# First GEMM behind each norm with two weight panels (three in the differential layer) interleaved by k tile

## What is computed

```python
for l in range(DEPTH):                       # 4
    mod = silu(cond) @ w_mod[l] + b_mod[l]   # 6 vectors of 1024 per conditioning
    h = rmsnorm(x, g_norm1[l]) * (1 + mod[1]) + mod[0]
    x = x + mod[2] * mixer_l(h)              # 0 MLA, 1 differential, 2 GQA, 3 RG-LRU
    h = rmsnorm(x, g_norm2[l]) * (1 + mod[4]) + mod[3]
    gte, up = split(h @ w_ffn_in[l])         # 2 x 2816 columns
    x = x + mod[5] * ((silu(gte) * up) @ w_ffn_out[l])
```

## Time and profile before

| | |
|---|---|
| three runs | 3645.62, 3646.51, 3653.01 us |
| profiled execution, its time | 3648.95 us |
| its span | 3646.3 us |
| granted clock of TensorE, mean | 0.959 |
| PE busy | 3323.3 us (91%) |
| PE weight loads busy | 3018.5 us (83%) |
| DVE, ACT, POOL busy | 1915.9 (53%), 1115.1 (31%), 217.2 us (6%) |
| HBM | 298.49 MB read, 83 GB/s over the span |

### The profile page before, as it was taken

How to read it: one execution, slowest core, us unless ns; L and a number is a source line. 1 busy time by engine, 2 the same in 40 slices (tenths; PEclk the granted TensorE clock), 3 DMA queues, 4 the chain that set the end, 5 groups by cost and what they waited for, 6 DMA issues and landing times.

```text
span 3646.3 us, 53064 instructions
## 1 busy us (share of the span) xinstructions
PE 3323.3 (91%) x20320; PEld 3018.5 (83%) x20320; DVE 1915.9 (53%) x2728; ACT 1115.1 (31%) x1734; POOL 217.2 (6%) x120
## 2 busy tenths in 40 slices
PE   7978898999989998899999688899999776899999
PEld 2556677999987775799999566799999676899999
DVE  2133346757355665585844345575754688533332
ACT  1334433211134554321111334331111455321111
POOL 0311100000000000000000310000000342000000
PEclk9989999999999998999999899899999888999999
DMA  7300014443221110253522100163522211222222
GB/s 264 104 18 16 21 35 133 133 161 121 75 71 41 41 43 15 83 187 104 179 72 70 49 23 12 47 196 107 188 80 67 56 51 40 58 75 73 77 70 80
DMA packets 421859, 304.08 MB, mean 83 GB/s; under 512 B 12019, under 2 KB 389494, under 8 KB 421622
## 3 DMA queue, kind: packets, MB, share of 16 engines
q1 hardware_dynamic: 411412, 293.23, 26.2%
q10 hardware_dynamic: 10338, 9.41, 0.8%
HBM read 298.49 MB, written 4.10 MB: 83 GB/s over the span
## 4 chain that ended last, share of the span: by engine, by line
PE 81%; DVE 6%; ACT 6%; DVEq 2%; issue 2%; ACTq 1%; DMA 1%; SPq 0%
PE psB L295 29%; PE psA L295 29%; PE psD L295 7%; PE psC L358 3%; PE psA L339 2%; PE psC L311 2%; PE psC L350 2%; PE psB L339 2%; ACT h_hi L1339 1%; PE psA L729 1%; ACT work L1336 1%; DVE work L2216 1%; PE psB L729 1%; ACTq L1338 1%; ACT work L397 1%
## 5 line engine op out<-in xcount | busy, mean ns | idle before, releaser
L1357 ACT ACTIVATE w_hi<-raw 128x1024 fp32r<-128x1024 f32 (+1 forms) x307 | 317.3, 1035 | 1160.3 <-PE psB L295 766.3
L1870 DVE TENSOR_TENSOR w_lo<-raw,w_hi 128x1024 fp32r<-128x1024 f32 (+1 forms) x307 | 365.3, 1191 | 347.6 <-ACT w_hi L1357 347.1
L295 PE MATMUL psA<-h_hi,w_hi 128*128 128x320 f32 x1616 | 384.2, 320 | 71.9 <-DVE h_lo L1941 60.3
L295 PE MATMUL psA<-h_lo,w_hi 128*128 128x320 f32 x1616 | 375.2, 314 | 0.0
L295 PE MATMUL psA<-h_hi,w_lo 128*128 128x320 f32 x1616 | 375.1, 314 | 0.0
L295 PE MATMUL psB<-h_hi,w_hi 128*128 128x320 f32 x1616 | 368.4, 309 | 0.0
L295 PE MATMUL psB<-h_lo,w_hi 128*128 128x320 f32 x1616 | 368.2, 309 | 0.0
L295 PE MATMUL psB<-h_hi,w_lo 128*128 128x320 f32 x1616 | 368.2, 309 | 0.0
L295 PEld LDWEIGHTS psA<-h_hi,w_hi 128*128 128x128 f32 x1616 | 273.5, 192 | 91.8 <-issue 43.7
L1900 DVE SCALAR_TENSOR_TENSOR work<-work,silu_c 128x1024 f32<-128x1024 f32 x252 | 312.5, 1281 | 12.4 <-issue 0.9
L295 PEld LDWEIGHTS psA<-h_lo,w_hi 128*128 128x128 f32 x1616 | 277.0, 192 | 0.0
(11 more groups left out here) (288 smaller groups left out, 5367.6 us busy)
## 6 DMA issues: line engine op xcount, KB each, us to landing
raw<-in_w_ffn_in SPq DMA_DIRECT2D x176, 512.0 KB, 4.0
work<-in_w_mod SPq DMA_DIRECT2D x144, 512.0 KB, 4.8
raw<-in_w_ffn_out SPq DMA_DIRECT2D x64, 512.0 KB, 3.9
work<-in_w_mod SPq DMA_DIRECT2D x12, 2048.0 KB, 7.9
raw<-in_w_ffn_out SPq DMA_DIRECT2D x32, 384.0 KB, 3.4
raw<-in_diff_w_in SPq DMA_DIRECT2D x24, 512.0 KB, 3.8
raw<-in_lru_w_in SPq DMA_DIRECT2D x16, 512.0 KB, 4.6
raw<-in_gqa_w_in SPq DMA_DIRECT2D x12, 512.0 KB, 3.8
```

Of the source, the lines that this page charges most:

```text
L295: last = nc.tensor.matmul(out[:, b, 0:half], w[slot][:, kt * cols + c0:kt * cols + c0 + P], r[:, o:o + half], start=(kt == 0 and p == 0), ...
L1357: nc.scalar.activation(w_hi[s][:, 0:n], raw[s][:, 0:n], ACT.Copy).then_inc(hi_done, 1)
L1870: nc.vector.tensor_tensor(w_lo[s_][:, 0:n], raw[s_][:, 0:n], w_hi[s_][:, 0:n].bitcast(F32), ALU.subtract).then_inc(split_done, 1)
```

## The change

PE issues the same products. Where the GEMM stands behind a norm, its output tiles are taken together: for each k tile PE waits once for `h_done` and then does six products of the first tile, six of the second (and six of the third in the differential layer), each tile in its own PSUM tile and with its own weight slot. What each tile waited for (its panel, its PSUM tile) is now waited for ahead of the first product. In the differential layer q, k and v of head 0 go to psD, psA and psB, and the steps on q and k follow after all three; ACT reads k and v from there, and moves the high parts of the next head's panels ahead of `kout` and `kcache`. Nothing else moves: SP, POOL and DVE have the order they had.

```diff
+        def fresh_products(pe, tiles, n):
+
+            for _, _, before in tiles:
+                before()
+            last = [None] * len(tiles)
+            for kt in range(KT):
+                pe.wait_ge(h_done, n * KT + kt + 1)
+                for k, (out, slot, _) in enumerate(tiles):
+                    last[k] = products(pe, out, slot, KT, P, 0, h_hi, h_lo, 0, T, TH, range(kt, kt + 1))
+                    if kt == KT - 1:
+                        last[k].then_inc(gemm_done, 1)
...
-                    for t in range(6):
-                        if t >= 2:
-                            acts.wait(pe, f"m{t - 2}")
-                        h_tile(psum[t % 2], "mla_in", t // 2, t % 2, 0 if t == 0 else None).then_inc(gemm_done, 1)
+                    fresh_products(pe, [(psum[j], j, lambda j=j: take_panel(pe, "mla_in", 0, j)) for j in range(2)], 0)
+                    for t in range(2, 6):
+                        acts.wait(pe, f"m{t - 2}")
+                        h_tile(psum[t % 2], "mla_in", t // 2, t % 2).then_inc(gemm_done, 1)
...
                     h0 = Head(0, 0)
-                    gq(h0, 0, 8)
-                    gk(h0, 0, 2)
+                    fresh_products(pe, [(psum[(3, 0, 1)[j]], (2, 0, 1)[j],
+                                         lambda j=j: pe.wait_ge(split_done, phases["diff"].of_head(h0, j, 3)))
+                                        for j in range(3)], 2)
                     ssq(h0)
-                    gk(h0, 2, 8)
                     acts.wait(pe, "rsq", h0)
                     rotq(h0)
-                    gv(h0, 0, 2)
                     ssk(h0)
-                    gv(h0, 2, 5)
                     acts.wait(pe, "rsk", h0)
                     rotk(h0)
-                    gv(h0, 5, 7)
                     kturn(h0)
-                    gv(h0, 7, 8)
                     acts.wait(pe, "kcache", h0)
+                    acts.wait(pe, "evv", h0)
                     scores(h0, 0)
...
                     for j in range(2):
-                        h_tile(psA, "gqa_kv", j, 0, 4 if j == 0 else None).then_inc(gemm_done, 1)
-                        h_tile(psB, "gqa_kv", j, 1).then_inc(gemm_done, 1)
+                        if j == 0:
+                            fresh_products(pe, [(psum[k], k, lambda k=k: take_panel(pe, "gqa_kv", 0, k)) for k in range(2)], 4)
...
                     def block_products(i, fresh):
...
+                        if fresh is not None:
+                            fresh_products(pe, [(psum[j], (2, 0)[j], lambda j=j: take_panel(pe, "lru", 0, j))
+                                                for j in range(2)], fresh)
...
                     if ch == 0:
-                        hidden_tile(0, 2 * layer + 1)
+                        pe.wait_ge(silu_done, base + 1)
+                        pe.wait_ge(hidden_done, base + 1)
+                        pe.wait_ge(x_done, x_tiles[0])
+                        fresh_products(pe, [(psum[j], j, lambda j=j: take_panel(pe, f"in{layer}.0", 0, j))
+                                            for j in range(2)], 2 * layer + 1)
...
-                    for step in (cached, evq, rsq, evk, rsk, kout, kcache):
-                        step(h0)
+                    cached(h0)
+                    evq(h0)
+                    rsq(h0)
+                    evk(h0, psA)
+                    rsk(h0)
                     high(Head(0, 1), 0)
+                    kout(h0)
                     high(Head(0, 1), 1)
-                    evv(h0)
+                    kcache(h0)
+                    evv(h0, psB)
                     exp(h0, 0)
```

More of the change, by code:

```diff
@@ L277, in build, with products @@
         LRU_DVE = Steps(sem("lru_dve"), ["m", "u", "h", "g", "o"], 5)
-        def products(pe, out, slot, kts, cols, c0, rhs_hi, rhs_lo, at, stride, half, part=None,
-                     fresh=None, before_last=None):
+        def products(pe, out, slot, kts, cols, c0, rhs_hi, rhs_lo, at, stride, half, part=None, before_last=None):
             last = None
             for kt in part or range(kts):
-                if fresh is not None:
-                    pe.wait_ge(h_done, fresh * KT + kt + 1)
                 if before_last and kt == kts - 1:
@@ L815, in _, with h_tile @@
                 norm(2 * layer)
-                def h_tile(out, name, i, j, fresh=None):
+                def h_tile(out, name, i, j):
                     slot = take_panel(pe, name, i, j)
-                    return products(pe, out, slot, KT, P, 0, h_hi, h_lo, 0, T, TH, fresh=fresh)
+                    return products(pe, out, slot, KT, P, 0, h_hi, h_lo, 0, T, TH)
                 if layer == 0:
@@ L980, in project_head @@
                             pe.wait_ge(split_done, phases["diff"].of_head(h, j, 3))
-                        last = products(pe, psD, (2, 0, 1)[j], KT, P, 0, h_hi, h_lo, 0, T, TH, part,
-                                        fresh=2 if isinstance(h.i, int) and (h.i, h.k, j) == (0, 0, 0) else None)
+                        last = products(pe, psD, (2, 0, 1)[j], KT, P, 0, h_hi, h_lo, 0, T, TH, part)
                         if part[-1] == KT - 1:
@@ L986, in gq @@
                     def gq(h, k0, k1):
-                        if k0 == 0 and h is not h0:
+                        if k0 == 0:
                             acts.wait(pe, "evv", h.last())
@@ L1198, in block_products @@
                     def block_products(i, fresh):
-                        LRU_ACT.wait(pe, "trb", i - 1)
-                        h_tile(psA, "lru", i, 0, fresh).then_inc(gemm_done, 1)
-                        LRU_ACT.wait(pe, "t", i - 1)
-                        h_tile(psB, "lru", i, 1).then_inc(gemm_done, 1)
+                        if fresh is not None:
+                            fresh_products(pe, [(psum[j], (2, 0)[j], lambda j=j: take_panel(pe, "lru", 0, j))
+                                                for j in range(2)], fresh)
+                        else:
+                            LRU_ACT.wait(pe, "trb", i - 1)
+                            h_tile(psA, "lru", i, 0).then_inc(gemm_done, 1)
+                            LRU_ACT.wait(pe, "t", i - 1)
+                            h_tile(psB, "lru", i, 1).then_inc(gemm_done, 1)
                         slot = take_panel(pe, "lru", i, 2)
@@ L1230, in _, with hidden_tile @@
                     base = layer * (FFN // P) + sum(FFN_CHUNKS[:ch])
-                    def hidden_tile(i, fresh):
+                    def hidden_tile(i):
                         pe.wait_ge(x_done, x_tiles[0] - 1)
                         pe.wait_ge(silu_done, i + (base + 1))
-                        h_tile(psA, f"in{layer}.{ch}", i, 0, fresh).then_inc(gemm_done, 1)
+                        h_tile(psA, f"in{layer}.{ch}", i, 0).then_inc(gemm_done, 1)
                         pe.wait_ge(hidden_done, i + (base + 1))
@@ L1245, in _ @@
                         with pe.Fori(start, end) as i:
-                            hidden_tile(i, None)
+                            hidden_tile(i)
                         mod_turn(*mod, k)
@@ L1513, in rsk, with evv @@
                         acts.mark(rstd(act, dsq_k, psC, 64, TH), "rsk")
-                    def evv(h):
+                    def evv(h, ps=psD):
                         act.wait_ge(gemm_done, phases["diff"].of_head(h, 2, 3))
                         dves.wait(act, "k", h)
-                        acts.mark(nc.scalar.activation(halves(dvt, TH), psD[:, :, 0:TH], ACT.Copy), "evv")
+                        acts.mark(nc.scalar.activation(halves(dvt, TH), ps[:, :, 0:TH], ACT.Copy), "evv")
                     def kout(h):
```

7 lines of the change are left out of this document (5 added, 2 removed).

## The result

| | before | after |
|---|---|---|
| median of 20 runs each, us | 3648.95 (3639.63 to 3655.73) | 3656.23 (3649.35 to 3661.21) |
| ratio, 95% interval | 1 | 1.0017 (1.0011 to 1.0024) |
| span of the profiled execution, us | 3646.3 | 3651.4 |
| mean granted clock of TensorE | 0.959 | 0.954 |

The change costs 0.17%, 6.2 us (4.0 to 8.8) by the ratio and 7.3 us by the medians. Measured once more beside other kernels it cost 0.21% (0.10 to 0.32), 7.7 us. Forecast was +8.8.

What follows compares the result with a forecast made beforehand. PE holds 81% of the last-ending chain; two-tile stages behind norms are partly paced by the norm. Terms 1.2 + 2.1 + 1.2 - 2.2 + 1.5 + 5.0 = +8.8 us on 3646.5 gave 3655, range 3643 to 3665.

Steps and rivals of the forecast that it cites:

- How much earlier PE is through: Two-tile stages behind a norm: PE through in 16.5 us instead of 21.2, 4.7 earlier, with 5.3 us at half clock.
- What a restart costs: Tile behind a PE wait of 3.5 us or more: about 2.2 us lost to half clock.
- MLA, +1.2: MLA, n = 0: tile 2 starts 1.0 us sooner, held by POOL's split, then a 2.2 us restart; sum +1.2.
- FFN in layers 0 to 2, +2.1: Hidden tile 1 starts unmoved behind the panel load; restarts of 2.2 each replace 1.65, 2.69 and 0.1; sum +2.1.
- FFN in layer 3, +1.2: Last FFN, n = 7, without modulation loads: hidden tile 1 starts 1.0 us sooner, restart +2.2; sum +1.2.
- GQA, -2.2: GQA, n = 4: next tile starts 4.4 us sooner, restart +2.2; sum -2.2.
- RG-LRU, +1.5: RG-LRU, n = 6: ACT starts on psA 1.4 us later, DVE sharing with POOL adds 0.1; sum +1.5.
- Differential, +5.0: Differential layer, n = 2: bare q and k chain of 17.1 us adds 1.2, half clock in it 3.8; sum +5.0.
- the first rival: Differential chain absorbed: its 5.0 shrinks to about 0, sum +3.8, 3650 us; chance 0.28.
- the clock stays up through the waits: Rival: denser PE work holds full clock over the waits in MLA, FFN and differential chain; sum -8.0, 3638.5 us; chance 0.06.
- their 3.8 and 2.2: Forecast clock costs: 3.8 us at half clock in the differential chain, 2.2 us restart behind the GQA stage.
- Full cover: Rival: next panels are ready, all 4.7 us count in seven stages, 33 us, giving 3614; chance 0.03.

Runs made afterwards that it cites:

- the waits filled: Changed kernel plus filler products, results unused, behind the interleaved stage in the MLA layer and four FFNs: 0.9986 against the kernel before, 5.1 us below it.
- the queue order: Kernel before with the panels of hidden tile 1 queued ahead of the next modulation's weight loads on SP's queue: 0.9965, -12.8 us.
- The stage alone: Kernel before with only the GQA layer (n = 4) interleaved: 0.9993, -2.6 us by the ratio, -1.8 by the medians.
- the kernel with the queue order: Kernel before with hidden tile 1's panels queued ahead of the modulation loads, plus the GQA interleaving alone: 0.9958 against the kernel before.
- Filled: Changed kernel with filler products, results unused, between the products of the differential layer's chain: 1.0010 against the kernel before, +3.6 us.
- 2 to 3 by the runs: Changed kernel with the differential layer as before, run twice: 1.0012 (+4.4 us) and 1.0016 (+5.8 us) against the kernel before.
- with the panels in time: Hidden tile 1's panels queued ahead of modulation loads: changed kernel (interleaved) 0.9978, -8.0 us; kernel before (in sequence) 0.9965, -12.8 us.
- Moving the load: Changed kernel, differential layer as before, panels queued ahead of modulation loads, Silu table loaded in ACT's wait, no fillers: 0.9949, -18.6 us against the kernel before.

## Why the prediction was right

Forecast 3655 and 3643 to 3665, slower most likely; measured 3656.23. The mechanism held: the panels and splits behind the stage hold the next start, the new wait costs a restart, and the differential chain is bare. That the time was met within about 1 us is partly luck. The forecast added 8.8 us to a median of 3646.5 of three runs, and that of twenty is 3648.95; the change itself costs 6.2 to 7.7 us. The stages sum to +5.6 us in the first trace and not to +8.8: MLA, GQA and RG-LRU came out 1.2 to 1.5 us lower each than forecast, the last FFN 0.5 higher. Point by point:

- **How much earlier PE is through: near, with one term too large in half of the stages.** Forecast 16.5 us; in the MLA and the four FFN stages PE reached its wait between 15.6 us (layer 0: 600.69 - 8.86 - 576.24) and 16.9 us (layer 2: 2389.36 - 7.19 - 2365.25) behind the first product. I had put 5.3 us at half clock at the start of every stage, the mean of before. In the changed kernel it was 2.8 to 3.1 us in four stages (MLA, FFN of layers 0 and 1, RG-LRU) and 5.2 to 6.0 in the other four. The MLA stage and the FFN of layer 2, PE alone, from the first product to the clock's rise:

```profile
135.70:138.71 3.01, 3.01 (x11) 0.50 0.02 5
2365.25:2371.03 5.78, 5.78 (x22) 0.50 0.00 1
```

  In the second execution the MLA stage had 5.65 us and GQA 2.83, with the same instructions; what decides between the two lengths isn't shown.
- **What a restart costs: right.** Forecast 2.2 us behind a wait of 3.5 us or more; the five tiles above took 8.64 to 9.71 us (the window of the last stops one product short), 1.6 to 2.7 over 7.04, 2.4 in the mean, and with the waits filled the loss was gone. The Trainium skill (TensorE: Matmul & The Clock Gate, "HAM oscillation — how this bites in real kernels") names a DMA wait between bursts of products as what sends the array back to half clock each time; by this rule the lengthened waits for the panels had to cost. The trace agrees in the three FFNs that wait for a load: 8.86 us idle in layer 0, then clock 0.71.
- **MLA, +1.2: inside the spread.** The tile started 1.9 us sooner, not 1.0, and psA was through 14.9 us behind the first product, not 15.8, since the half clock at its start lasted 3.0 us and not 5.3. The sum came out at -0.3 in this execution. In the other, with 5.65 us at half clock at the start and a tile that began at half clock (9.64 us instead of 8.64), it was +1.9.
- **FFN in layers 0 to 2, +2.1: the sum is right, two parts less so.** The sum is +0.3 - 0.7 + 2.6 = +2.2. It holds because two errors cancel: the restarts cost 2.6, 2.7 and 2.6 us and not 2.2 each, which makes +3.5 instead of +2.1, and the starts moved by -0.7, -0.7 and +0.1 us, where the forecast had 0. In layer 0 those 0.7 us are the load itself, 7.39 us instead of 8.09. That SP's queue sets the start is shown by the queue order, which moved it to 21.20.
- **FFN in layer 3, +1.2.** +1.7 in one execution, -0.3 in the other. The start was 0.9 us sooner (forecast 1.0).
- **GQA, -2.2.** The stage alone gave -1.8 to -2.6 by the runs, with intervals that take in 0. The trace of the changed kernel has -3.4, since its tile met full clock (7.3 us; 8.9 in the second execution, where the start came 4.8 us sooner); my 4.4 sooner and 2.2 restart are what the kernel with the queue order shows (4.2 and 2.0).
- **RG-LRU, +1.5: too high.** Measured +0.25. The step that failed is ACT's start on psA, taken as 1.4 us later: it was 0.5 later (14.9 us against 14.4), for PE was at half clock for 3.1 us and not for 5.3. DVE's part held: its steps behind the first took 8.12 + 0.49 + 0.83 = 9.44 us against 4.80 + 2.08 + 2.81 = 9.69, beside POOL operations that now follow each other directly. The block of 74 products behind it then ran 1.25 us shorter, at a clock of 0.86 instead of 0.77; from its first product to the next norm's the layer was 2.5 us shorter in this execution and 0.4 in the other.
- **Differential, +5.0: right, and for the reasons given.** +5.1: a chain of 21.0 us where I had 17.1 + 3.8. Filled, it took 17.5 at full clock. How much of the 5 us reaches the end seems smaller: 3.6 to 4.3 by segments, 2 to 3 by the runs. Whether a part of the first rival (the chain is absorbed later) holds is not told by runs whose intervals overlap.
- **The rivals.** That the clock stays up through the waits did not happen; with fillers it does, and the kernel is 5.1 us faster than before. I had priced this at 8.0; the fillers left the differential chain and the tile behind GQA alone, and less their 3.8 and 2.2 that is 2.0, which lies inside the measured 1.8 to 8.4. Full cover fell for the reasons that the rows gave.

DVE's convolution and split before, and in the changed kernel, with the earlier trace rows:

```profile
2878.47 4.80 DVE L2216 SCALAR_TENSOR_TENSOR work<-work,vecs 128x644 f32<-128x644 f32 x3
2883.35 2.08 DVE L446 CAST y_hi<-work 128x644 fp32r<-128x644 f32 x1
```

```profile
2883.55 8.12 DVE L2237 SCALAR_TENSOR_TENSOR work<-work,vecs 128x644 f32<-128x644 f32 x3
2891.74 0.49 DVE L455 CAST y_hi<-work 128x644 fp32r<-128x644 f32 x1
2892.31 0.83 DVE L457 TENSOR_TENSOR y_lo<-work,y_hi 128x644 fp32r<-128x644 f32 x1
```

## What to carry to other kernels

Before making an engine finish a stage sooner, follow the chain of what it does next: here a load, a split and a table load held the next tile, and the work that was packed tighter had been the cover of that wait. On TensorE a packed stage followed by one long wait can be worse than the same work spread out, since the clock falls and the next tile pays: with the panels in time, stage and tile of layer 0 took 30.07 us interleaved and 28.30 in sequence. So free the successor first (queue order, table load, order of the split), and only then interleave. If a wait remains, products with no use can keep the clock; in the FFN of layer 0 they cost no time, since PE would have been idle anyway.

## What the hardware showed that I had not expected

- 20 to 54 useless products in a wait were worth 2.5 us of the next FFN tile each time, 11 us of the kernel in all (5.1 us below before instead of 6.2 above).
- A wait of 2.2 to 2.3 us between busy stretches was enough to lose 1.5 us in three FFNs of one execution and cost nothing in the fourth, while a wait of 2.67 us in the kernel before (FFN of layer 2) cost nothing; the length of the wait alone does not decide. A whole stage varies too: the same instructions took 28.14 and 30.33 us in two executions of the changed kernel.
- The clock can fall while PE works: MLA tile 2 of the changed kernel began at 1.00 and was at half clock from 0.75 to 4.2 us behind its start.
- The table load for Silu is 1.28 us and the Silu follows 0.01 us behind it (3180.29, 3181.58). The Trainium skill (ScalarE: Activation LUTs, "What ACT_TABLE_LOAD costs") gives about the same for the load and adds a drain of 1.38 us. No such gap stands in these rows, where ACT had been idle ahead of the load, nor behind the norm n = 6, where the load follows ACT's work directly (work from 2881.64 for 0.45 us, load at 2882.11, next work at 2883.40). Moving the load gained 1.3 us (20.26 to 18.98). The measurement decides, for the load alone.
